# Eight single transfers in place of four pairs in a state mixer's schedule, and a later start of what follows

## The reference

```
h  = rms_norm(x) ;  columns of h @ w_in -> fq fk fv fg ff su sg mq mg
fox = attention(rms(fq), rms(fk), fv, decay from log_sigmoid(ff)) * silu(fg)      8 heads x 64
ssm = S5(su)                                            * silu(sg)      16 groups x 16 channels
mem = attention(rms(mq), 256 memory tokens)             * silu(mg)      4 heads x 64
y  = x + concat(fox, ssm, mem) @ w_out
```

## Time and profile before

| what | us |
|---|---|
| median of three runs | 1490.5 (1489.8 to 1493.42) |
| profiled execution, device time | 1492.01 |
| its span in the trace | 1490.3 |
| TensorE busy (matmul) | 1421.2, 95% of the span |
| VectorE busy | 933.6, 63% |
| ScalarE busy | 743.0, 50% |
| GpSimd busy | 285.7, 19% |

### The profile page before, as it was taken

How to read it: one execution, slowest core, us unless ns; L and a number is a source line. 1 busy time by engine, 2 the same in 40 slices (tenths; PEclk the granted TensorE clock), 3 DMA queues, 4 the chain that set the end, 5 groups by cost and what they waited for, 6 DMA issues and landing times.

```text
span 1490.3 us, 28755 instructions
## 1 busy us (share of the span) xinstructions
PE 1421.2 (95%) x10222; PEld 1170.9 (79%) x10222; DVE 933.6 (63%) x1942; ACT 743.0 (50%) x1764; POOL 285.7 (19%) x344
## 2 busy tenths in 40 slices
PE   7999999999999989999999999999999999899998
PEld 7998767788877767777777878878778787778886
DVE  3679755691566787655335666666666666576664
ACT  5656422422434464444334666766666667732221
POOL 1111332100043242210001110101000002445542
PEclk9999999999999999999999999999999999999999
DMA  7776599986279587879975763370733601365552
GB/s 220 234 267 231 189 272 241 321 252 197 91 183 344 177 255 252 264 249 280 322 268 138 215 146 86 80 152 17 161 73 79 135 16 36 99 223 186 188 187 82
DMA packets 211373, 276.06 MB, mean 185 GB/s; under 512 B 73696, under 2 KB 147840, under 8 KB 207744
## 3 DMA queue, kind: packets, MB, share of 16 engines
q1 hardware_dynamic: 210192, 274.22, 62.6%
q10 hardware_dynamic: 1040, 0.00, 0.0%
HBM read 186.93 MB, written 86.00 MB: 183 GB/s over the span
## 4 chain that ended last, share of the span: by engine, by line
PE 54%; DVE 5%; issue 4%; ACT 4%; DMA 2%; POOL 2%; SPq 1%; ACTq 0%; DVEq 0%; POOLq 0%
PE in_g L924 13%; PE attn_pv L2459 10%; PE attn_s L2524 8%; PE attn_t L2443 6%; PE attn_s L2424 4%; PE attn_s L2427 3%; PE attn_pv L2524 3%; ACT attn_probs L2557 2%; DVE attn_tops L2725 2%; PE in_b L1099 1%; POOL in_hv L1796 1%; PE in_b L1051 1%; DVE attn_probs_turned L2738 1%; PE in_b L1154 1%; DMA attn_out<-scratch_mem_gate 1%
## 5 line engine op out<-in xcount | busy, mean ns | idle before, releaser
L924 PE MATMUL in_g<-in_wh,in_xh 128*128 128x512 f32 (+2 forms) x904 | 332.0, 380 | 12.5 <-DVE in_z L1535 5.0
L924 PE MATMUL in_g<-in_wl,in_xh 128*128 128x512 f32 (+2 forms) x904 | 321.8, 369 | 0.0
L2725 DVE TENSOR_REDUCE attn_tops<-attn_s 128x1 f32<-128x512 f32 (+3 forms) x288 | 173.0, 619 | 129.7 <-PE attn_s L2427 129.4
L2557 ACT ACTIVATE attn_probs<-attn_s,attn_negmax 128x512 f32<-128x512 f32 (+3 forms) x384 | 227.3, 604 | 33.4 <-DVE attn_negmax L2729 33.1
L924 PE MATMUL in_g<-in_wh,in_xl 128*128 128x512 f32 (+2 forms) x904 | 234.7, 378 | 0.5 <-DVE in_xl L1518 0.3
L924 PEld LDWEIGHTS in_g<-in_wh,in_xh 128*128 128x128 f32 x904 | 165.5, 189 | 49.1 <-issue 17.4
L2443 PE MATMUL attn_t<-all_ident,attn_probs 128*128 128x128 f32 x1216 | 189.4, 274 | 8.2 <-ACT attn_probs_turned L2567 5.9
L924 PEld LDWEIGHTS in_g<-in_wl,in_xh 128*128 128x128 f32 x904 | 165.6, 189 | 28.0
L924 PEld LDWEIGHTS in_g<-in_wh,in_xl 128*128 128x128 f32 x904 | 157.9, 189 | 33.7 <-issue 5.2
L2443 PEld LDWEIGHTS attn_t<-all_ident,attn_probs 128*128 128x128 f32 x1216 | 145.9, 141 | 42.5 <-ACT attn_probs L2557 11.4
L2459 PE MATMUL attn_pv<-attn_probs_turned,attn_v 128*64 128x128 f32 x2176 | 134.6, 275 | 0.7 <-DVE attn_out L2762 0.7
(11 more groups left out here) (350 smaller groups left out, 2484.3 us busy)
## 6 DMA issues: line engine op xcount, KB each, us to landing
in_xu<-scratch_xt SPq DMA_DIRECT2D x87, 512.0 KB, 5.4
in_xl<-scratch_xt SPq DMA_DIRECT2D x34, 512.0 KB, 4.5
in_raw<-in_w_in SPq DMA_DIRECT2D x40, 256.0 KB, 6.0
scratch_xt<-in_xu SPq DMA_DIRECT2D x19, 512.0 KB, 5.4
scratch_xt<-in_xl SPq DMA_DIRECT2D x17, 512.0 KB, 6.2
scratch_k<-in_x_turned SPq DMA_DIRECT2D x17, 512.0 KB, 6.6
scratch_q<-in_x_turned SPq DMA_DIRECT2D x17, 512.0 KB, 5.4
in_x_turned<-in_x_prompt SPq DMA_DIRECT2D x16, 512.0 KB, 5.2
```

Of the source, the lines that this page charges most:

```text
L924: last = X.matmul(g_ps[b][:, 0:m], x, ws[:, c, w0:w0 + m], start=(c == 0 and h == 0 and ws is wh), stop=(c == KC - 1 and h == 1))
L2557: last = F(probs[:, s % 2, i, at:at + n, :], s_ps[g % RING][:, at:at + n, :], ACT.Exp, bias=negmax[:, s % 2, top:top + 1], accum_out=total)
L2725: V.tensor_reduce(tops[:, s % 2, i:i + 1], bank[:, 0:n, :].rearrange("p n k -> p (n k)"), AX.X, ALU.max).then_inc(s_top, 1)
```

## The change

`s5_u` becomes eight entries of one transfer (entries 11 to 18), `s5_toep` eight entries of one transfer (28 to 35), and everything from `s5_drive` on stands three entries later (`at += 12` in place of 9), so `main` has 139 entries. Instructions, bytes, tiles and waits are otherwise the same.

```diff
-    for n in range(4):
-        main.put(at + 2 + 2 * n, "s5_u", n)
+    for n in range(8):
+        main.put(at + 1 + n, "s5_u", n)
...
-    for n in range(4):
+    for n in range(8):
         main.put(at + 1 + n, "s5_toep", n)
-    at += 9
+    at += 12
     for g in range(GROUPS // 2):
         main.put(at + g, "s5_drive", g)
...
                 if what == "s5_u":
+                    s = n[0]
                     sp.wait_ge(s_bounce, 32)
-                    for s in (2 * n[0], 2 * n[0] + 1):
-                        sp.dma_start(u[s * CH:(s + 1) * CH, :, :], D.ssm_in[s, :, :].rearrange("(g q) j -> q g j", q=CH))\
-                            .then_inc(s_uin, 16)
+                    sp.dma_start(u[s * CH:(s + 1) * CH, :, :], D.ssm_in[s, :, :].rearrange("(g q) j -> q g j", q=CH))\
+                        .then_inc(s_uin, 16)
...
                 if what == "s5_toep":
                     sp.wait_ge(s_kdone, 1)
                     sp.wait_ge(s_zeroed, 4)
-                    for s in (2 * n[0], 2 * n[0] + 1):
-                        sp.dma_start(toep[s * CH:(s + 1) * CH, :, s * CH:], kern[:, :, 0:(L - s) * CH]).then_inc(s_toep, 16)
+                    s = n[0]
+                    sp.dma_start(toep[s * CH:(s + 1) * CH, :, s * CH:], kern[:, :, 0:(L - s) * CH]).then_inc(s_toep, 16)
```

## The result

The changed kernel takes 1509.24 us (median of four runs, 1508.46 to 1510.26) against 1491.24 (1489.8 to 1493.42) for the kernel before in runs beside it: ratio 1.0122, 95% interval 1.0109 to 1.0136, so 18.0 us slower. Two executions, one of e4_late_memq (2301.89 us) and one of the kernel before beside e1 to e4 (3545.17 us), were far slower than all others of their kernel and are left out of every ratio. The forecast was 1502.0, +11.5 us, with the inner range ending at 1508 and the wide one at 1510. The sign and the two places were right.

The account below looks back on a forecast made before the run. TensorE bounds the kernel (54% of the span), in keys waiting on VectorE and full DMA engines. 2.9 - 1.1 + 8.4 + 1.9 - 0.6 = +11.5 us gives 1502.0; range 1497 to 1508, wide 1492 to 1510.

Parts of the forecast that it names:

- 1. Keys and values: Keys: three drives now run behind the `in_xl` load at 1.2 us each, less 0.7: +2.9 us, bounds -6.6 and +3.6.
- 2. Start of queries: From visit 51: half of TensorE's 2.2 us wait on `stage` goes: -1.1 us, bounds -2.2 and +1.5.
- 3. The end of `main`: In memkv: VectorE stands for the last mixer store, memq's low weights behind it: +8.4 us, bounds +7.8 and +10.3.
- 4. The clock: Around visit 70: TensorE runs at half clock after standing about 8 us: +1.9 us, bounds 0 and +3.8.
- 5. After that: From memq on: later `late` costs 0, the decay sums' wait has half a chance to vanish: -0.6 us.
- the sample steps collide: Rival, chance 0.10: a 1.5 us wait in each of eight samples, +10.5 us more: 1512.
- The queue is not the gate: Rival, chance 0.12: in keys `in_xl` lands early, -6.6 us there: +2.0 in all, 1492.5.
- The spill costs nothing: Rival at memkv, store lands before VectorE arrives: -7.7 us, 1482.8, chance 0.06; or 1491.7 if the gate holds, 0.05.
- The change does not do what it says: Rival, chance 0.07: transfers stay bunched because SP is held in issue; drives still three slots later: 1502.7.

Follow-up runs that it names:

- e4_late_memq: Changed kernel with the first six `late` entries allowed from memq on in place of memkv: 1499.7 us, ratio 1.0050.
- e1: Changed kernel with three idle entries behind the scan taken out, so `main` has 136 entries and no spill: 1498.52 us, ratio 1.0047.
- f1: Kernel before with only the `u` inputs as eight single transfers at entries 11 to 18: 1495.06 us, ratio 1.0028.
- e5: Kernel before, transfers in pairs, drives three entries later, three idle entries behind the scan taken out, so no spill: 1494.92 us, ratio 1.0019.
- e2: Kernel before, transfers in pairs, with the drives and all behind them three entries later, spill included: 1503.06 us, ratio 1.0077.
- e7: Kernel before with three more idle entries behind the scan, so only the end of `main` spills into memkv: 1500.83 us, ratio 1.0062.
- f2: Kernel before with three more idle entries behind the scan, and the first six `late` entries allowed from memq on: 1490.03 us, ratio 0.9990.
- the trimmed kernels: The two kernels e1 and e5, with three idle entries behind the scan taken out: ratios 1.0047 and 1.0019.
- e3: Changed kernel with the drives back at their old entries, single transfers kept, no spill: 1498.41 us, ratio 1.0045.
- e8: Kernel before with the two `w_glu` loads moved from entry 27 to entry 60: 1490.6 us, ratio 0.9996.
- e6: Kernel before with the `u` inputs as eight single transfers at entries 12 to 19: 1492.23 us, ratio 1.0007.

## Why the prediction came out as it did, point by point

**1. Keys and values: forecast +2.9, measured +7.9 in the trace and +7.0 in time (e1).** The bounds ended at +3.6, so this step failed, and in one sentence. I counted that "one or none more than before" stands ahead of each `xu` load, and concluded only that the waits on kernel reads do not go. The count was right and its price was left at zero. One transfer of 272 KB more ahead of the load of visit 28 made it 2.5 us later, the wait 2.6 us longer, and the products behind it slow for 2.5 us. Alone it is +4.2 us (f1). Rows 4 already had the DMA engines full there; in a full queue a place is a price.

The part on the drives held in size. From visit 28 to 36 the changed kernel loses 2.9 us more, and the late drives alone cost 2.8 us (e5). But its terms were not the ones I named. Counted from the gate, the drives are 3 x 1.2 = 3.6; in place of the 0.7 us sooner, `in_xl` came 2.5 us later, since SP issued it at 268.68 in place of 265.60, 4.1 us later counted from visit 22 (it then took 7.2 us in place of 8.8); and behind the 3.6 us stand the clock was at 0.54 in 277 to 280 us, some 1.6 us. That is 7.7 of the 7.9. And that TensorE gets through visits 32 and 33 without the drive waits was true only because it came late: with pairs, 2.3 of the 3.2 us came back there (e5), and even the changed kernel waits 1.0 us for `in_wl` at the start of visit 34. The last spread kernel was forecast at 267.7 and landed at 269.1. The row on the clock that I used for memkv alone had a bound here ("if the stand before `in_xl` counts as well"); it did count.

**2. Start of queries: forecast -1.1.** The waits on `stage` fell from 2.2 to 1.0 us, and visit 58 is 1.3 us better against visit 36. But from visit 58 to 68 the changed kernel loses 1.4 us, and e2, e7 and f2, whose mixer also ends three entries later, 0.6 to 1.2; e1 and e5, where it does not, 0.2 or less. There TensorE's waits in the glu products (L1051) go from 2.5 to 3.3 us in the changed kernel and visits 62 to 65 change places of work; which of these makes the rest was not tried. The net is 0.

**3. The end of `main`: forecast +8.4, measured +7.2 at the start of visit 70.** The mechanism held. VectorE stood 8.33 us ahead of L1676, released by the store. The store was issued 8.1 us behind the first weight load (forecast 7.7) and took 7.9 us (row used: 7.2). The fit of the Trainium skill (DMA: Bandwidth & Descriptors, Anatomy of one DMA), which the page gives for transfers that GpSimd issues, makes an estimate of 4.6 us for this size. The store that SP issued here took 3.3 us more. The low weights of memq begin at 550.16 in place of 534.11, 9.1 us later once the 7.0 us lost by visit 68 are taken off. By the start of visit 70 TensorE has lost only 7.2 us more than at visit 68, and 9.0 by visit 73. So "TensorE has no slack to give" was wrong by 1.9 us: the 1.1 us wait of the earlier trace rows was for `in_xh`, and before visit 70 began 2.7 us behind the first low weight, now 0.9.

**4. The clock: forecast +1.9.** Visit 70 took 8.99 us where 7.11 were needed before: +1.9, with the granted clock at 0.50 in the stretch of 553 to 556 us. The place and the size held. By their spacing the nine slow products alone cost some 1.9 us; a wait of 1.0 us for `in_xl` came into the visit, and a wait of 0.45 us for `in_wl` and four transposes (L1059) dropped out of it, so the rest cancels. What I missed is that the same price falls due at visits 27 and 34.

**5. After that: forecast -0.6, measured +1.0 from visit 73 to 103 and +0.4 in the second stage.** The spill alone gives the same +1.0 (e7), with the same wait of 1.5 us on `smp_turned` (L1712) that the kernel before does not have; the trimmed kernels have 0. The wait of the decay sums did not vanish (1.4 us). The bounds held, the value did not.

**The sum.** From the table: 7.9 to visit 36, 0.1 to visit 68, 9.0 to visit 73, 1.0 to visit 103, and 0.4 in the second stage are 18.4. This execution was 1.0 us ahead at visit 22, which leaves 17.4, the difference of the two profiled executions. Against the forecast, step 1 was too low by 5.0, step 2 by 1.2, step 5 by 2.0, and steps 3 and 4 together too high by 1.3. From single parts in time, `u` 4.2 (f1), late drives 2.8 (e5) and spill 9.2 (e7) are 16.2 of 18.2; each has an interval some 3 to 5 us wide, so the rest can't be told from nothing. The spread kernels as singles were never run alone; e3 less f1 is 2.5 us, with the drives at their old places. That the time stayed inside the wide range, by 0.8 us, was luck: the inner range, worked out from the bounds, ended at 1508, no working is given for the 1510, and step 1 was past its bound by 4.3. The rival *the sample steps collide* had 10 us for what were 1.0.

**The other rivals.** *The queue is not the gate*: TensorE stood for `in_xl` and passed it at 275.95, so no. *The spill costs nothing* would have needed a store below 1 us: 7.9. (Its sum of -7.7 leaves out the -0.6 of step 5.) *The change does not do what it says*: SP's rows show the singles apart, and where they were apart they did harm.

## What to carry to other kernels

Where the DMA engines are full, write down for each load that someone waits on how many transfers stand ahead of it, before and after. One more of 272 KB was 2.6 us of waiting, and the clock behind the wait doubled it. Behind a wait that goes, look for the load that it hid. Where an in-order list ends with a store that a later step waits on, look at what is queued behind that wait: eight weights behind it made a free spill cost 10 us, and the same wait behind the weights cost nothing. A gain read from one trace at one place (e8, 2.7 us) counts only at the end of the stage, and only beyond what unchanged kernels scatter there (2.1 us).

## What the runs showed of the hardware

The clock. Idle times of TensorE of 3.5 us and more were each followed by slow products: 3.54 us (f1: eight products of L990 in 1.47 us), 3.57 and 4.20 us (granted 0.54 and 0.50), 7.93 us (0.50). The start of the kernel before is among them by its durations, though 1.00 is written there. Shorter ones went either way. At visits 32 and 33, 2.27 (e2) and 2.32 us (e5) were followed by 0.50 within 3 us, and 2.06 us (e6) by 1.00. Before L990 at visit 27, waits of 1.94 (e2), 1.92 (e6) and 1.88 us (e7) were followed by a granted clock of 1.00, one of 1.84 us (e5) by 0.72 in 224 to 230 us. The 1.74 us ahead of L1066 in e8 were followed by 0.60. The length of the one gap does not decide it there, and what does was not tried. The Trainium skill (TensorE: Matmul & The Clock Gate, Why this matters for your kernels) says that idle gaps bring the lower clock. The traces agree, and show a price of 1.5 to 2.5 us on top of the longer stands.

SP. A single DMA issue took up to 6.3 us of SP's time with the engines full (186.58 in the changed kernel). Where in such a queue a transfer is listed therefore also sets when the next ones are issued at all.
